# A transformer block on eight cores: turning the attention result of each 128-token tile by a transposing DMA instead of by TensorE

## The reference

```
h   = modulate(layer_norm(x), shift, scale)
q, k, v, u, vb, ga, gb = split(h @ w_in)
ya  = window_attention(rope(q), rope(k), v, kc, vc, sink)   # 8 heads of 64, 2 key heads, blocks of 128,
                                                            # keys: 3 blocks around, 256 context tokens, one sink
yb  = gelu(u) * (w_s @ layer_norm(gelu(vb)) + b_s)          # per chunk of 128 tokens
mix = (sigmoid(ga) * (ya @ w_a) + sigmoid(gb) * (yb @ w_b)) @ w_o
x1  = layer_norm(alpha * x + gate1 * mix)
out = layer_norm(alpha * x1 + gate2 * swiglu(modulate(layer_norm(x1))))
```

## Time and profile before

| what | value |
|---|---|
| median of 3 runs | 956.18 us (954.79, 956.18, 971.96) |
| profiled execution, its own time | 954.09 us |
| span of its slowest core (core 4) | 952.5 us; the eight cores 949.5 to 952.5 |
| TensorE busy | 885.8 us, 93% of the span |
| VectorE busy | 636.9 us, 67% |
| ScalarE, GpSimd busy | 304.8 and 304.3 us, 32% each |
| bytes moved by DMA | 88.10 MB, mean 92 GB/s |

### The profile page before, as it was taken

The page is one execution under the profiler, slowest core; times in us unless marked ns, Lnnn a source line. Parts: engine busy times, 40 slices in busy tenths (PEclk is TensorE's granted clock), DMA queues, the critical chain, the costliest instruction groups (busy, mean ns, idle before and its releaser), DMA issues.

```text
span 952.5 us, 15652 instructions; the slowest of 8 cores (949.5 to 952.5 us)
## 1 busy us (share of the span) xinstructions
PE 885.8 (93%) x5477; PEld 436.1 (46%) x5477; DVE 636.9 (67%) x1126; ACT 304.8 (32%) x477; POOL 304.3 (32%) x235
## 2 busy tenths in 40 slices
PE   1399699998999999999997999999999999999995
PEld 1335445354555444444443444444444444444672
DVE  5338787876664766766799655565656674666787
ACT  0434666656775244424333311111111111111110
POOL 6027676375453333333345020120202011111111
PEclk9689999999999999999999999999999999999998
DMA  8996830299773410168655250412303020111112
GB/s 210 190 198 191 173 105 13 78 155 167 125 121 99 147 23 12 23 140 120 150 151 152 62 103 31 89 31 59 89 1 89 1 45 1 45 45 66 45 69 87
DMA packets 47276, 88.10 MB, mean 92 GB/s; under 512 B 19808, under 2 KB 20064, under 8 KB 45536
## 3 DMA queue, kind: packets, MB, share of 16 engines
q0 software_dynamic: 18064, 34.54, 23.6%
q1 hardware_dynamic: 29136, 52.56, 17.7%
HBM read 109.05 MB, written 8.39 MB: 123 GB/s over the span
## 4 chain that ended last, share of the span: by engine, by line
PE 87%; DMA 5%; DVE 3%; issue 2%; POOL 1%; ACT 1%; SPq 0%; POOLq 0%; DVEq 0%; ACTq 0%
PE psum L1189 30%; PE psum L1215 15%; PE psum L1036 12%; PE psum L1053 6%; PE psum L1088 6%; DMA arena<-wqk 4%; PE psum L678 4%; PE psum L734 3%; PE psum L916 3%; PE psum L956 2%; PE psum L765 2%; DMA arena<-xh 1%; DVE arena L496 1%; DVE arena L1099 1%; PE psum L468 1%
## 5 line engine op out<-in xcount | busy, mean ns | idle before, releaser
L1189 PE MATMUL psum<-arena 128*128 128x512 bf16 (+1 forms) x1536 | 316.1, 361 | 3.1 <-DVE arena L505 3.1
L1189 PEld LDWEIGHTS psum<-arena 128*128 128x128 bf16 x1536 | 150.2, 98 | 158.8 <-issue 3.6
L1195 ACT ACTIVATE arena<-psum 128x512 f32<-128x512 f32 (+1 forms) x96 | 53.9, 561 | 370.5 <-PE psum L1189 370.4
L1215 PE MATMUL psum<-arena 128*128 128x512 bf16 x704 | 164.0, 379 | 2.5 <-DVE arena L1225 1.8
L1229 DVE TENSOR_TENSOR arena<-arena,psum 128x512 f32<-128x512 f32 x224 | 140.7, 680 | 19.2 <-PE psum L1215 19.2
L509 POOL TENSOR_TENSOR arena<-arena 128x1 f32<-128x1 f32 (+1 forms) x74 | 73.7, 997 | 240.4 <-DVE arena L507 236.8
L1198 DVE TENSOR_TENSOR arena<-psum,arena 128x512 bf16<-128x512 f32 (+1 forms) x96 | 61.9, 645 | 127.7 <-PE psum L1189 125.3
L1036 PE MATMUL psum<-arena 128*128 128x512 bf16 x512 | 117.5, 379 | 2.5 <-DVE arena L1058 2.5
L496 DVE BATCH_NORM_STATS2 arena<-arena 128x6 f32<-128x512 f32 x152 | 99.6, 685 | 17.6 <-DMA arena<-xh 9.1
L1215 PEld LDWEIGHTS psum<-arena 128*128 128x128 bf16 x704 | 68.4, 98 | 85.4 <-issue 6.2
L925 ACT ACTIVATE arena<-psum 128x1024 bf16<-128x1024 f32 (+1 forms) x100 | 81.1, 853 | 19.3 <-PE psum L916 14.3
(11 more groups left out here) (101 smaller groups left out, 940.3 us busy)
## 6 DMA issues: line engine op xcount, KB each, us to landing
arena<-xh SPq DMA_DIRECT2D x34, 512.0 KB, 7.8
arena<-wada POOLq DMA_DIRECT2D x24, 512.0 KB, 11.3
arena<-wff POOLq DMA_DIRECT2D x11, 1024.0 KB, 10.2
arena<-wff SPq DMA_DIRECT2D x11, 1024.0 KB, 7.2
out<-arena SPq DMA_DIRECT2D x15, 512.0 KB, 2.6
arena<-wc POOLq DMA_DIRECT2D x8, 768.0 KB, 19.8
arena<-wout SPq DMA_DIRECT2D x8, 512.0 KB, 4.3
arena<-rope SPq DMA_DIRECT2D x4, 512.0 KB, 7.3
```

The costliest lines, as they stand in the source:

```text
L1189: ins = e.matmul(bank(ps)[:, 0:n], lhsT=w1v[r][:, k, lo:lo + 128], rhs=h2(k), start=(k == 0), stop=(k == 7))
L1195: s = P.op('act', prio - 150, act_cost(n), lambda e: e.activation(out=sgv(), in_=bank(pg)[:, 0:n], func=AF.Silu), after=[a], takes=[sg], g ...
L1215: ins = e.matmul(bank(ps), lhsT=actv[(r, fi, t)], rhs=w2v[r][:, fi, h * 512:(h + 1) * 512], start=(n == 0), stop=(n == 2 * len(rounds) - 1))
```

## The change

The four TensorE transposes, their PSUM bank and the VectorE copy of each attention tile are replaced by one transposing DMA, SBUF to SBUF, on SyncE's queue, from `yatm` to the same place in `qv`. It comes after the tile's two normalisations and the last score matmul of the tile, and it is now what gives back the `yatm` buffer. The semaphore of each such transfer belongs to the buffer that it reads, so its name is known only after the plan is made; hence the key is a function. The planner's model of transfers gets rates of its own for the case that such a transfer and a transfer of GpSimd's queue are both active (21 GB/s and 300 GB/s).

```
-                rate = 320e3 if len(live) == 1 else 150e3
-                step = min([rest[e] / rate for e in live] + [c - t for c in coming])
+                rate = {e: 320e3 if len(live) == 1 else 150e3 for e in live}
+                if len(live) == 2 and not isinstance(flights['sp'][at['sp']][1].key, str):
+                    rate = {'sp': 21e3, 'pool': 300e3}
+                step = min([rest[e] / rate[e] for e in live] + [c - t for c in coming])
                 t += step
                 for e in live:
-                    rest[e] -= step * rate
+                    rest[e] -= step * rate[e]
...
-                    k = 'd_' + o.key
+                    k = 'd_' + (o.key if isinstance(o.key, str) else o.key())
...
-        tb = banks(*X)
-
-        def ft(e):
-            for c in range(4):
-                ins = e.transpose(bankb(tb)[:, c * 128:(c + 1) * 128], V(L['yatm'] + KB * sid(ytm), BF16, 512)[:, c * 128:(c + 1) * 128], ident)
-            return ins
-        tr = P.op('pe', prio + 0.7, 0.28, ft, after=norms, takes=[tb], gives=[ytm])
-        t_ya[j] = P.op('dve', prio + 0.7, 0.42, lambda e: e.tensor_copy(
-            out=qv[:, :, jt * 128:(jt + 1) * 128], in_=bankb(tb)[:, 0:512].rearrange('p (a b) -> p a b', a=4)),
-            after=[tr, q_last], gives=[tb])
+        t_ya[j] = P.dma('sp', prio + 0.7, 128, lambda e: e.dma_start_transpose(
+            out=qv[:, :, jt * 128:(jt + 1) * 128], in_=V(L['yatm'] + KB * sid(ytm), BF16, 512)), lambda: 'ya%d' % sid(ytm),
+            after=norms + [q_last], gives=[ytm])
```

## The result

The changed kernel takes 1.0052 times as long as the one before, 95% interval 1.0039 to 1.0064: about 5 us slower, where 4 to 5 us faster was forecast. By the bound of 2% that is no change. By the interval it is a small loss, and the forecast had the wrong sign. The profiled execution took 959.39 us (954.09 before); with the other four behind the ratio it is 959.39 to 961.89, above the forecast's range of 944 to 959.

What follows compares the result with a forecast made beforehand. TensorE's instruction stream was taken to bound the kernel. Terms: -5.2 removal, 0 elsewhere, 0 waiting, +1 displaced loads = -4.2 us, giving 949.9 from 954.09 or 950.8 from 955.0; 950.2 taken, range 944 to 959 us.

Steps and rivals of the forecast that it cites:

- the removal: TensorE's stream in attention: 16 tiles' transposes and their waits gone, 5.2 us saved, bounds 3.7 and 5.5.
- The remade order: Whole program, rebuilt by the planner: small holes may open and close, 2 us allowed either way.
- One thing sits in that queue: SyncE's queue during attention: only the norm-weight load at 290.89 named; tiles near it have 10 us to spare.
- The landing beside loads: Attention tiles among full DMA engines: a half-size transpose lands in about 6 us, at most 10.3.
- the buffers become the bound: Rival, attention result's two buffers: landings above 10.6 us delay VectorE's normalisations; at 16 us, +15.6 us; chance 0.08.
- half the packets and so half the turns: DMA queues beside a load: half-size transpose waits through half the packet turns, landing in some 6 us.
- VectorE's copies: VectorE in attention: 16 copies, 6.7 us of work, removed off the path; 0 counted, bounds 0 and 2.5 us.
- (a): Merge of a tile group: group 0's last landing, at 207 even after 10.3 us, is hidden before use at 213.74.
- The displaced modulation weights: Loads issued at 223, full DMA engines: transposes delay them, TensorE may wait 0 to 3.5 us, 1 taken.
- (c): First two groups' residual loads, after the last tile: 1.5 to 2 us later, 0 counted, bound 2.
- The quiet landing: Transposing DMA of 128x512 without a load beside it: lands in 2.5 us.
- given back to late loads: Rival, attention stretch: 3.5 us of load slips waited out, remade order costs 2 more, 954.4 us; chance 0.21.

Runs made afterwards that it cites:

- e3: Kernel before with its old instruction order, TensorE transposes and VectorE copies removed and nothing in their place; ratio 0.9953, stretch 322.8 us.
- before: The kernel without the change, with TensorE transposes and VectorE copies; profiled execution 954.09 us, stretch 325.8 us, the base of all ratios.
- e11: e9 with the transposing DMAs of tiles 3 to 6 left out, all orders else kept; ratio 0.9962, stretch 324.1 us.
- e9: Changed kernel with only VectorE's eight output-weight products and SyncE's loads of these weights moved as early as in before; ratio 1.0017, stretch 327.4 us.
- after: The changed kernel as first measured against before; ratio 1.0052, profiled execution 959.39 us, stretch 330.2 us.
- e10: The changed kernel run again with nothing altered; ratio to before 1.0069, stretch 331.8 us.
- e2: Changed kernel in its own order, without the last two of the eight output-weight loads; ratio to before 0.9960, stretch 324.2 us.
- e12: e9 run again with nothing altered; ratio to before 0.9993, stretch 327.4 us.
- e6: Kernel before, no transposing DMA in attention, second output-weight product forced behind tile 2's second normalisation and plan remade; ratio 1.0057, stretch 329.3 us.
- e4: Changed kernel with the planner's old transfer rates, everything else as changed; no ratio, two executions of 963.21 and 964.61 us, stretch 331.4 us.
- e1: Kernel before with its old instruction order, transposes dropped and the transposing DMA put in place of the copy; ratio 0.9995, stretch 324.3 us.

## Why the prediction was wrong

The differences in microseconds of stretch, on the median core: the removal -3.0 (e3 against before); the new order as repaired, without the transposes of tiles 3 to 6, +1.3 (e11 against e3); those transposes, among full DMA engines, +3.3 (e9 against e11); the late loads +3.6 (after and e10 against e9, mean of 2.8 and 4.4). These differences share their ends, so that their sum, +5.2, is the mean of the measured +4.4 and +6.0 by construction; it confirms nothing. Two of them need a word. The +1.3 is about the 1.4 us that TensorE waits for L698, the price of the repair and not of the change; without it the late loads would come to about 5 us, nearer to e2, which is 6.0 us shorter than the changed kernel (it also moves 1 MB less). And the +3.3 shows only where the late loads are mended: in after TensorE waits for L479 on one core alone, for 0.4 us, while in e2, e9 and e12 it does so on all, for 1.0 to 2.8. What the loaded transposes would cost in the changed kernel by themselves no run separates. The last two terms, each larger than the whole gain, are what the forecast lacked.

**The step that failed** is "The plan's new rates only change the order in which the program is written ... I allow 2 us either way for it". The remade order was treated as a small symmetric unknown. What the runs show in its place is one definite thing: the second product is placed some 20 us later, and that costs 3.6 us, or about 5 without the price of the repair, by a chain of two buffers that the trace of before already held: loads that land in 3.6 to 5.4 us, the last issued at 191.9, just ahead of a stage with a DMA share of up to 1.09. The prediction's "One thing sits in that queue" overlooked these eight loads in SyncE's queue. I asked which operations wait for the new transfer, and never which transfers already in that queue have no room to be late. This was shown from both sides: e6 (the product's later place, with the order that follows from it, is sufficient) and e2 and e9 (without the late loads the hole is gone). The loss does not need the rates that I named (e4).

**The landing beside loads** was the second failure, a term sized too low: about 6 us taken, 10.3 as the upper end, 10.6 as the point from which buffers bind. With the engines full the half-size transposes landed in up to 14.3 us in after, 14.8 in e1 and 15.3 in e9. The 10.3 was no upper end, and the trace of before says why. The load of the earlier trace rows, issued at 435.18, has this time to landing:

```profile
DMA to landing us min/median/max: 12.3/12.3/12.3
```

So it landed at 447.5, and the transpose of the earlier trace rows at 448.4, right behind it. On the eight cores of before all 24 transposing DMAs of L1110 that were issued with one or two of GpSimd's loads in flight landed 0.7 to 1.1 us behind the last of them. Such a landing tells how much of the loads was left, so neither the excess in proportion to the data nor "half as large" could be read from it. Those of e1 on core 1, the three issued from 225 to 240 us with four to seven such loads in flight, then the six from 246 to 281 with one or two:

```profile
DMA to landing us min/median/max: 12.7/12.8/12.8
```

```profile
DMA to landing us min/median/max: 4.2/6.1/8.8
```

The 6 us fit the second group; the first took twice that. The mechanism was right (rival "the buffers become the bound"). Its threshold held for the old order: in e1 VectorE waits 0.4 to 2.3 us a time for landings of 11.9 to 14.2, so 11 to 13 us were free. The new order leaves less: where VectorE waits, at tile 6 for the landing of tile 4, landing less wait is about 8 us on every core, 10.3 - 2.4 in after and 13.1 - 4.9 in e9. The Trainium skill ("DMA: Bandwidth & Descriptors", section "Queues, rings and completion order") has the engines take turns between queues packet by packet; my inference from it, half the packets and so half the turns, the trace does not bear out, since with one or two loads in flight the landing follows the loads' end. The rule in "VectorE: DVE Perf Modes" of the Trainium skill (section "Rules for kernel authors") that I set against the change, TensorE for a 128x128 transpose where PSUM will do, is borne out so far as the DMA gained nothing that can be told from zero (e1, 0.9995).

**The removal** was sized at 5.2 us with 3.7 as its lower end; the stretch gives 3.0. The time as a whole gives 0.47%, 4.5 us, with an interval of 2.8 to 6.2 that includes both. The price of a block was read too high. It was the distance from the block to the matmul behind it, but that matmul keeps a part of this distance when the block is gone. The gate matmuls ahead of the block at 245.28, core 4 of before (the rest is in the earlier trace rows), and the same place on core 1 of e3:

```profile
243.55 1.90 PE L1036 MATMUL psum<-arena 128*128 128x512 bf16 x8
```

```profile
243.05 1.90 PE L1039 MATMUL psum<-arena 128*128 128x512 bf16 x8
244.88 0.60 PE L917 MATMUL psum<-arena 64*128 64x512 bf16 x4
```

With the block the scores start 245.60 - 243.55 = 2.05 us behind the first gate matmul, without it 1.83: the block costs 0.22 and not 0.32. On core 1, by the same comparison, 14 of the 16 blocks cost 0.22 to 0.25 us and the two that also waited for VectorE 0.49 and 0.55, in all 4.2. Of this some 1.3 us are lost again in e3: TensorE waits 0.4 us for VectorE's L696, which it did not before, and longer for ScalarE's exponentials, on core 4

```profile
PE psum L917 <- ACT arena L926: 1.8, 5, 0.6
```

against 0.9 us before. So some of the freed time only moves to the next engine that is late.

**What held.** VectorE's copies gave nothing: the hole of the earlier trace rows stayed at 2.5 us in e3. Group 0's merge was hidden, as in (a). The displaced modulation weights, bounds 0 to 3.5 and 1 taken, are what e1 shows, 0 to 3.4 us by core. The residual loads in (c) were later than I said, VectorE waited 5.2 us and not 2, but no wait of TensorE followed, so the 0 stands. The quiet landing, 2.5 forecast, was 2.4. The rival "given back to late loads" was right in kind and wrong in name: not the modulation weights but the output weights were late; and its 3.5 + 2 us are less than the two prices, 3.3 + 3.6. In the old order, which removes the failed step, the forecast of -4.2 would still have been too good: e1 has -0.05%, interval -0.22 to +0.12%, some -0.5 us.

**Open:** the whole of the difference between a hole of 7.6 us, with matmuls at half the clock behind it, and the 3.6 us of stretch that it costs. Parts are seen: the repaired order waits elsewhere (1.4 us at L680, 1.1 to 2.8 at L1048), and it has slow matmuls elsewhere, with a granted clock of 0.72 from 190 to 195 us on core 4 of e9, where the changed kernel has 1.00 from 190 to 200. Open is also why the last stage is 4 us longer on some cores.

## What to carry to other kernels

Before moving work onto a queue, list what already stands in it, and when each item must land at the latest; a load that lands 5 us after issue just before the DMA engines fill up has no slack, and a change anywhere ahead of it in a chain of two buffers can push it over that edge. Where a scheduler rebuilds the order, that order is part of the change: test it apart from the change itself, by substituting the new operation into the old plan and by forcing the new order's one suspicious placement on the old kernel. A landing measured beside a load may be no more than the load's own: compare the two before scaling it by the transfer's size, and ask how many loads will be queued at the new place. And the price of a block in an engine's stream is the distance between its neighbours with it, less that without it.

## What was not expected of the hardware

The same 128x512 transposing DMA took 2.4 us from issue to landing with the engines idle and 12.0 to 14.8 us with them full (e1, all cores, issued from 190 to 235 us): more than the 10.3 us of one of twice the size beside a feed-forward load, which landed right behind that load. The 512 KB loads of SyncE's queue went from 3.6 to 5.4 us to 13.3 to 14.4 us when they were issued 3.5 us or more behind three loads of GpSimd's queue. And the clock fell within the hole: TensorE had no instruction from 207.6 to 215.2, and in stretches of 5 us, columns as in the earlier trace rows, its granted clock was

```profile
205.00:210.00 5.00, 2.59 (x12) 0.98 (x10) 0.17 (x1) 0.60 (x1) 3.15 (x4) 1.00 1.10 277
210.00:215.00 5.00, 0.00 (x0) 0.00 (x0) 2.95 (x4) 0.00 (x0) 0.56 (x1) 0.60 1.07 187
215.00:220.00 5.00, 4.44 (x18) 1.58 (x20) 3.92 (x7) 1.27 (x3) 2.82 (x4) 0.50 1.06 169
220.00:225.00 5.00, 5.00 (x37) 2.17 (x34) 3.40 (x6) 4.77 (x5) 3.03 (x3) 0.87 1.09 167
```

full ahead of the hole, 0.60 within it, 0.50 (1.2 GHz) for the 5 us in which work came back, and 0.87 in the next. That is why the eight matmuls at 216.2 took 3.57 us.
